# Decoder step: last rows, index projection, both scorings, projections and selection as one stage of interleaved streams

## The reference

```python
h = _rmsnorm(x, p['norm_mix'])
proj = h @ p['w_in']
q, k, v, q_idx, k_idx, w_idx, rw, gate_a, gate_b = _split(proj, SPLIT_SIZES)
...
def _indexer_scores(q_idx, w_idx, k_idx):
    dots = jnp.einsum('bthd,bsd->bths', q_idx, k_idx).astype(jnp.float32)
    w = w_idx.astype(jnp.float32) * IDX_SCALE
    return jnp.einsum('bths,bth->bts', jax.nn.relu(dots), w)
...
past_idx_k = cache_idx_k[page_table].reshape(b, past, IDX_DIM)
all_idx_k = jnp.concatenate([past_idx_k, k_idx.astype(past_idx_k.dtype)], axis=1)
scores = _indexer_scores(q_idx, w_idx, all_idx_k)
scores = jnp.where(causal[None], scores, -jnp.inf)
_, sel = lax.top_k(scores, topk)
...
return x, k, v, k_idx, wkv_new, h[:, -1]
```

## Time and profile before

| what | value |
|---|---|
| median of 3 runs | 3078.86 us (3068.66 to 3085.59) |
| profiled execution, its own time | 3064.48 us |
| its span | 3062.7 us |
| mean granted TensorE clock | 0.904 |
| TensorE busy | 2546.5 us, 83% of the span |
| VectorE busy | 1477.4 us, 48% |
| ScalarE busy | 547.5 us, 18% |
| projection matmuls (L322) | 1248 records, 390.1 us busy |
| counts of the search (L768) | 180 records of the prompt's tiles, 170.3 us busy |

### The profile page before, as it was taken

How to read it: one execution, slowest core, us unless ns; L and a number is a source line. 1 busy time by engine, 2 the same in 40 slices (tenths; PEclk the granted TensorE clock), 3 DMA queues, 4 the chain that set the end, 5 groups by cost and what they waited for, 6 DMA issues and landing times. The chain is left out here.

```text
span 3062.7 us, 52996 instructions
## 1 busy us (share of the span) xinstructions
PE 2546.5 (83%) x21845; PEld 1844.2 (60%) x21845; DVE 1477.4 (48%) x2991; ACT 547.5 (18%) x1139; POOL 76.8 (3%) x120
## 2 busy tenths in 40 slices
PE   4645889994778788787857787799999999999998
PEld 3324556662454555555535454477888888888886
DVE  2142099996427236163344454467554353443443
ACT  3020000001223022231233343321210010000101
POOL 0000000001000000000010010000000000000000
PEclk7865999997988889879879889999999999999999
DMA  3111332223212223132166556353111111111111
GB/s 117 37 48 41 109 112 71 71 64 105 82 44 83 61 59 84 46 86 55 27 208 207 164 186 222 101 201 113 42 40 39 39 38 40 41 41 42 42 42 66
DMA packets 281095, 253.69 MB, mean 83 GB/s; under 512 B 52395, under 2 KB 231181, under 8 KB 280742
## 3 DMA queue, kind: packets, MB, share of 16 engines
q1 hardware_dynamic: 206430, 192.74, 20.4%
q10 hardware_dynamic: 74440, 57.74, 6.4%
HBM read 201.84 MB, written 48.59 MB: 82 GB/s over the span
## 5 line engine op out<-in xcount | busy, mean ns | idle before, releaser
L322 PE MATMUL ps_pr<-hT,w_pr 128*128 128x384 f32 (+1 forms) x1248 | 390.1, 476 | 21.4 <-DMA w_pr<-in_w_in 21.4
L322 PEld LDWEIGHTS ps_pr<-hT,w_pr 128*128 128x128 f32 x1248 | 239.5, 192 | 172.0 <-issue 17.1
L1014 PE MATMUL rwkv_banks<-h_chunk,w_gate 128*128 128x384 f32 (+1 forms) x768 | 290.6, 523 | 18.7 <-ACT gate_rows L1355 8.5
L2497 DVE TENSOR_TENSOR x<-x,ps_mm 128x272 f32<-128x272 f32 x280 | 120.9, 436 | 308.0 <-PE ps_mm L2464 307.9
L2464 PE MATMUL ps_mm<-merged_then_hidden,w_mm 128*128 128x272 f32 x960 | 227.1, 393 | 1.6 <-DVE sums_of_right_sides L2714 0.9
L1014 PEld LDWEIGHTS rwkv_banks<-h_chunk,w_gate 128*128 128x128 f32 x768 | 152.9, 210 | 111.0 <-issue 46.6
L2464 PEld LDWEIGHTS ps_mm<-merged_then_hidden,w_mm 128*128 128x128 f32 x960 | 182.2, 190 | 39.9 <-DVE sums_of_right_sides L2714 1.3
L2464 PE MATMUL ps_mm<-v_T_and_gates_then_h_mlp,w_mm 128*128 128x272 f32 x864 | 204.5, 392 | 0.0
L2488 ACT COPY merged_then_hidden<-ps_mm 128x272 f32<-128x272 f32 x160 | 61.5, 385 | 723.4 <-PE ps_mm L2464 723.4
L2464 PEld LDWEIGHTS ps_mm<-v_T_and_gates_then_h_mlp,w_mm 128*128 128x128 f32 x864 | 164.1, 190 | 33.9
L768 DVE TENSOR_SCALAR_CACHE_REDUCE above<-scores,mid 128x384 f32<-128x384 f32 (+1 forms) x180 | 170.3, 946 | 6.4
(11 more groups left out here) (437 smaller groups left out, 3794.8 us busy)
## 6 DMA issues: line engine op xcount, KB each, us to landing
k_pages<-in_cache_k SPq DMA_DIRECT2D x128, 256.0 KB, 3.1
v_pages<-in_cache_v SPq DMA_DIRECT2D x128, 256.0 KB, 3.9
w_gate<-in_w_in ACTq DMA_DIRECT2D x48, 512.0 KB, 4.2
w_mm<-in_w_mlp_in SPq DMA_DIRECT2D x32, 512.0 KB, 4.9
w_mm<-in_w_mlp_out SPq DMA_DIRECT2D x32, 512.0 KB, 4.8
proj_T<-stage_pr ACTq DMA_DIRECT2D x26, 548.0 KB, 4.0
w_pr<-in_w_in SPq DMA_DIRECT2D x25, 512.0 KB, 3.9
v_T_and_gates_then_h_mlp<-gates_T SPq DMA_DIRECT2D x16, 544.0 KB, 4.7
```

The lines of the kernel that those rows point to most:

```text
L322: ins = self.nc.tensor.matmul(self.ps[0:width, slot % 2, c, 0:m], w[:, k, 0:width], rhs[:, k, t0:t0 + m], start=(k == 0), stop=(k == slice ...
L1014: ins = MM(B[:, GB, 0:w], gw[:, n % 2, k, :], hc[:, k, 0:w], start=(k == 0), stop=(k == KO - 1))
L2497: self.nc.vector.tensor_tensor(to, to, ps, ALU.add).then_inc(self.by_dve, 1)
```

## The change

The five stages `shift_rows`, `project_index`, `score_new`, `score_past` and `project_and_select` become one, `project_score_select`, with one barrier at its end. Its parts on each engine are streams that `weave` puts into one order. The numbers are in steps of roughly a microsecond of projection work: CHUNK = 4.9 for a projection chunk, NEW = 46 for the first unit of the new keys and 0.75 for each further one, PASTS = 84 for the first sequence and 5 for each further one.

- All 29 projection blocks run in one series, the index key block first. They have two PSUM banks in place of two sets of three, and are copied out chunk by chunk (`made` and `kept` count chunks). A chunk is issued in two halves of 4 slices, between which other streams may step.
- The index key rows and index queries stay in SBUF (`kw`, `qi`); the keys for both halves of the partitions, and the small operands of the past scoring, still come back from `proj_T`.
- The units of the new keys are cut at 512 keys: 44 in place of 28, with a ring of four banks.
- All 128 index pages have a buffer of their own, and their loads wait for no earlier sequence; two of three are issued by SP, one of three by ACT. `ties` and `rank` of the selection reuse that memory.
- The pages of a sequence are turned in two groups of 4 transposes, each copied out by itself.
- The last rows are copied by ScalarE instead of VectorE. The bias products follow the first chunks; the store of `hT` is issued late in the stage.
- The loops are written out instead of running on the chip. The bisection loop on VectorE and the masks are as before, and come after all scoring on VectorE's queue.

```diff
-            p.stage(shift_rows, o["shift_prompt"], o["shift_sample"])
-            p.stage(project_index, a["w_in"])
-            p.stage(score_new, o["idxk_prompt"], o["idxk_sample"])
-            p.stage(score_past, a["cache_idx_k"], a["page_table"])
-            p.stage(project_and_select, a["w_in"], a["rel_bias"], one_hot)
+            p.stage(project_score_select, a["w_in"], a["rel_bias"], one_hot, o["idxk_prompt"], o["idxk_sample"],
+                    a["cache_idx_k"], a["page_table"], o["shift_prompt"], o["shift_sample"])
...
+    SLOTS, RING = 4, 4
+    pages = sb("idx_pages", [128, NB, NPG * 64])
+    flat = pages.rearrange("p b c -> p (b c)")
+    ties, rank = flat[:, 0:NKS], flat[:, NKS:2 * NKS]
+    B = p.ps("first_banks", [128, 8, 512], own)
+    blocks = [(col(W_KI, 68), 68, B_KI)] + [(col(W_QI + 128 * j), 128, B_QI + j) for j in range(2)]
+    units = [(i, h, c, min(512, (i + 1) * 128 - c)) for i in SEARCHED for h in range(IH)
+             for c in range(0, (i + 1) * 128, 512)] + [(NI, h, 0, TS) for h in range(IH)]
+    BY_ACT = [g for g in range(NPG) if g % 3 == 2]
+    BY_SP = [g for g in range(NPG) if g % 3 != 2]
+    CHUNK, NEW, ITEM, PASTS, BATCH = 4.9, 46.0, 0.75, 84.0, 5.0
...
+        @block.sync
+            def weights():
+                for n, (parts, _, _) in enumerate(blocks):
+                    yield -1.0 if n < SLOTS else 3 * CHUNK * (n - SLOTS + 1) + 0.2
+                    if n >= SLOTS:
+                        sp.wait_ge(S["made"], 3 * (n - SLOTS + 1))
...
+            def key_pages():
+                yield 0.0
+                sp.wait_ge(S["pt_in"], 16)
+                for n, (b, g) in enumerate((b, g) for b in range(NB) for g in BY_SP):
+                    yield 1.1 * n
+                    load_page(sp, b, g, 0)
+            def once():
+                yield -2.0
+                sp.dma_start(pt[:, :], page_table.rearrange("b (o g) -> o (b g)", o=1)).then_inc(S["pt_in"], 16)
+                yield -0.5
+                sp.dma_start(oh[:, :], one_hot).then_inc(S["nb_in"], 16)
+                sp.dma_start(rb[:, :], rel_bias).then_inc(S["nb_in"], 16)
+                yield 12.0
+                sp.wait_ge(S["last_kept"], 1)
...
+                yield 18.0
+                sp.wait_ge(S["kw_stored"], 16)
...
+                yield 26.0
+                sp.wait_ge(S["kw_rows"], 3)
...
+                yield NEW + 1.0
+                sp.wait_ge(S["q_stored"], 32)
...
+                yield PASTS + NB * BATCH + 20.0
+                sp.dma_start(p.h_d.rearrange("k p t -> p k t"), p.hT[:, :, 0:NT]).then_inc(S["h_kept"], 16)
+            weave(once(), weights(), key_pages())
...
+        @block.tensor
+            def project():
+                    for c, (t0, m) in enumerate(CHX):
+                        q = 3 * n + c
+                        for half in range(2):
+                            yield CHUNK * (q + 0.5 * half)
+                            if half == 0 and q >= 2:
+                                pe.wait_ge(S["kept"], q - 1)
+                            for k in range(4 * half, 4 * half + 4):
+                                ins = MM(B[0:width, 6 + q % 2, 0:m], wk[:, k, 0:width], p.hT[:, k, t0:t0 + m],
+                                         start=(k == 0), stop=(k == KO - 1))
...
+            def bias():
+                    yield 5.0 + 0.5 * n
...
+            def turn_last():
+                yield 10.0
...
+            def turn_kw():
+                    yield 17.0 + 1.2 * g
...
+            def dots_new():
+                for u, (i, h, c, n) in enumerate(units):
+                    yield NEW + ITEM * u
...
+                    if u >= RING:
+                        pe.wait_ge(S["relued"], u - RING + 1)
...
+            def past():
+                for b in range(NB):
+                    for half in range(2):
+                        yield PASTS + BATCH * b + 1.2 * half
+                        turn_pages(b, half)
+                    yield PASTS + BATCH * b + 3.0
+                    dots_past(b)
+                for q in range(NPG // 4):
+                    yield PASTS + BATCH * NB + 4.0 + 2.0 * q
...
+            weave(project(), bias(), turn_last(), turn_kw(), dots_new(), past())
...
+        @block.scalar
+            def keep():
+                    for c, (t0, m) in enumerate(CHX):
+                        yield CHUNK * (q + 1) + 0.05
+                        act.wait_ge(S["made"], q + 1)
...
+            def key_pages():
+                for n, (b, g) in enumerate((b, g) for b in range(NB) for g in BY_ACT):
+                    yield 1.2 * n
+                    load_page(act, b, g, 1)
+            def relu():
+                    yield NEW + ITEM * u + 0.3
+                    act.wait_ge(S["dotted"], u + 1)
+                    if u >= RING:
+                        act.wait_ge(S["added"], u - RING + 1)
...
+            def keep_keys():
+                        yield PASTS + BATCH * b + 1.2 * half + 0.6
...
+            weave(keep(), keep_last(), key_pages(), relu(), keep_keys())
```

More of the change, by code:

```diff
@@ L265, in _ @@
             chain_.wait()
[L268 to L333, removed]
@@ L336 @@
[L336 to L349, removed]
-        for c, (t0, m) in enumerate(d.chunks):
-            ins = self.nc.scalar.copy(self.stage[0:rows, b, t0:t0 + m], d.ps[0:rows, b, c, 0:m])
-            ins.then_inc(d.taken[b] if c == 2 else self.copied, 1)
-        act.wait_ge(self.copied, d.nth(n, 1) * 2 + 2)
-        act.wait_ge(d.taken[b], d.nth(n, 2, 1))
-        dst = self.p.proj[ds(block, 1), 0:rows, :].rearrange("b p t -> (b p) t")
-        act.dma_start(dst, self.stage[0:rows, b, :]).then_inc(self.stored[b], 16)
@@ new lines, in _ @@
+            MM = nc.tensor.matmul
+            def project():
+                loads = [0] * SLOTS
+                for n, (parts, width, _) in enumerate(blocks):
+                    loads[n % SLOTS] += len(parts)
+                    wk = w[:, n % SLOTS, :].rearrange("p (k c) -> p k c", k=KO)
+                    for c, (t0, m) in enumerate(CHX):
+                        q = 3 * n + c
+                        for half in range(2):
+                            yield CHUNK * (q + 0.5 * half)
+                            if c == 0 and half == 0:
+                                pe.wait_ge(w_ready[n % SLOTS], 16 * loads[n % SLOTS])
+                            if half == 0 and q >= 2:
[3 more added lines that the diff above has]
+                                         start=(k == 0), stop=(k == KO - 1))
+                        ins.then_inc(S["made"], 1)
@@ new lines, in turn_pages @@
+            def turn_pages(b, half):
+                if half == 0:
+                    pe.wait_ge(page_in[b][0], 16 * len(BY_SP))
+                    pe.wait_ge(page_in[b][1], 16 * len(BY_ACT))
+                if b == 0:
+                    pe.wait_ge(S["relued"], NU)
+                else:
+                    pe.wait_ge(S["kt_made"], 2 * b + half - 1)
+                for j in range(4 * half, 4 * half + 4):
+                    ins = nc.tensor.transpose(B[:, half, (j % 4) * 128:(j % 4) * 128 + 128],
+                                              pages[:, b, j * 128:j * 128 + 128], p.ident[:, :])
+                ins.then_inc(S["pages_turned"], 1)
@@ L575, in batch @@
                     o = s * 256 + (g // 2) * 32
-                    ins = nc.tensor.matmul(dots[:, g % 2, o:o + 32],
-                                           kt[r0:r0 + 64, s, (g // 2) * 128:(g // 2) * 128 + 128],
-                                           qws[r0:r0 + 64, s, 0:32], start=True, stop=True)
-                ins.then_inc(dotted, 1)
-            for s in range(2):
-                batch(s, s, 0)
-            with pe.Fori(1, NB // 2) as i:
-                for s in range(2):
-                    batch(i * 2 + s, s, i)
```

541 lines of the change are left out of this document (214 added, 327 removed).

## The result

The changed kernel took 2991.32 us in the median of 4 runs (2989.19 to 3000.68), the kernel before 3078.56 in 4. The ratio is 0.9721, with a 95% interval of 0.9696 to 0.9746: 87 us less, where 85 were forecast (2994). The profiled execution took 2992.02 us with a span of 2990.1, only 72.6 less than the profiled span of before. The stages after RWKV took 2.5 us less.

A forecast was written before the change was run, and what follows sets the result against it. VectorE's 345 us search, needing all scores and starting late, was taken to bound the region. 292.3 + 5.6 + 345.3 + 7.0 = 650.2 instead of 735.7, 85.5 us less, gives 2994 us on the median; forecast 2978 to 3010, wider range 2972 to 3034.

The forecast's parts named there:

- Start: First projection matmul, with weight loads issued straight behind the first barrier: at about 93 us instead of 98.3.
- The queue up to the last scores: TensorE's work before the last scores are turned back: 195.3 us plus 4 of small waits, ending at 292.3.
- a batch: Past scoring of one sequence on TensorE: 8 transposes 1.07 us, dots 1.8 (half the low-clock 3.62), together 2.9.
- batches 6 and 7: Last page batches, no half chunk between transposes and dots: TensorE waits for ScalarE's copy, twice about 1.0 us.
- the 55 half chunks: Projection work on TensorE's queue before the last scores: 2.46 us each, 135.1 in all, warm-up 1.9 apart.
- VectorE: After the last turn back: 5.6 us of copies, reductions and causal term, then the unchanged search of 345.3 us.
- The end of the stage: From the last mask to the next stage's first load: 7.0 us, as in the kernel before.
- TensorE's end: 119 half chunks left after the last scores take 293 us; TensorE ends at 585, 58 us short of being last.
- Queues that hand their waits to TensorE: Rival, in the scoring: one late copy stops all streams, about half the gain, 3034 us; 0.20 together with late pages.
- Pages that arrive late: Rival, in the batches: SP's weight waits gate page loads, 3014 to 3034 us; 0.20 together with queue waits.
- bank cycling: Rule against the forecast: changing PSUM banks every chunk idles TensorE, its clock swings, kernel slower; fallen-clock chance 0.04.
- A fallen clock: Rival, in the scoring part: all at 1.2 GHz makes 195 us 390, the time 3189 us; chance 0.04.

The follow-up runs named there:

- more_semaphores: The changed kernel with 40 more unused semaphores allotted to the stage, which its end clears: 2990.72 us in one run.
- the second trace: The changed kernel without an edit, measured again with a trace of a second execution: 2986.87 us, 0.9702 of the kernel before.
- twenty_rounds: The changed kernel with 20 rounds of bisection in place of 30: 2933.05 us, 0.9533 of the kernel before.
- scores_bare: The changed kernel with projection chunks from the tenth on moved behind the whole scoring: 2974.84 us, 0.9673 of the kernel before.
- one_per_batch: The changed kernel with other sort keys, 37 half chunks (not 55) before the last scores, one in each batch: 2944.81 us, 0.9566 of the kernel before.
- bias_first: The kernel before with all eight bias products made ahead of the first projection block: 3057.36 us, 0.9935 of the unedited one.
- pages_ahead: The kernel before with an index page buffer for each of the eight sequences: 3077.23 us, 0.9996 of the unedited one.
- fewer_between: The changed kernel with other sort keys, 43 half chunks (not 55) before the last scores: 2956.98 us, 0.9611 of the kernel before.

## Why the prediction was right

The mechanism is the one forecast: the search starts 84.8 us earlier, takes as long as before, and TensorE ends before it. By the prediction's steps, forecast against trace:

- **Start**: 93 against 90.68. The page table's load costs SP 0.25 us, and the first matmul follows the first weights' issue by 3.4 us instead of 5.0. That block has 68 columns in place of 128; whether that is the reason was not tried.
- **The queue up to the last scores**: 199.3 against 202.3, and its end 292.3 against 292.98, since it began 2.3 sooner. Its terms, from each group's start to the next one's: score matmuls 22.7 against 20.8, in the lower half of the bounds; a batch 2.9 against 2.8 (0.87 of transposes and 1.91 of dots), so halving the low-clock dots was right; bias 6.7 against 6.5; batches 6 and 7 wait 0.67 each, not 1.0; idle time 3.4 in all, where I took 6.0 in two terms. The term that I had too small is the one that looked surest. After the others the 55 half chunks take 145.7 us with the warm-up, where I had 137.0. Between other streams a half chunk takes 2.69 (384 columns, 228.29 to 230.98) or 2.30 (328), 2.56 in the mean of a block, not the 2.46 of the undisturbed stretch behind (119 in 292.25 us); that is 5.5 us. Dips of the clock, 0.97 in the mean of the stretch, are the rest. So this term was 8.7 us too small, and it was made up by the start (2.3), the idle time (2.6), the score matmuls (1.9) and some smaller ones. That the end came within 0.7 us of the forecast is luck.
- **VectorE**: 5.6 and 345.3 us against 5.6 (292.98 to 298.59) and 345.4.
- **The end of the stage**: 7.0 against 9.05. Here the step itself was incomplete: I took the old barrier's price, and it holds a clearing of semaphores whose number the change raises. more_semaphores shows the price.
- **The next stage**: 650.2 against 653.05, and 655.6 in the second trace.
- **TensorE's end**: 585 against 585.06, and its 58 us of room against the 61 us that twenty_rounds took out.

The forecast of 2994 was made on the median. The sum on the single profiled execution, 2979, is 13 us below the 2992 that the profiled execution took; 2.9 of that are the region, most of the rest the RWKV stage's spread, which had been at its short end in the trace of before (808.0). The forecast range is not the one that its bounds give: dots 6 either way and waits from -4 to +21 around 2994 are 2984 to 3021, not 2978 to 3010. The measured time lies in both.

**The rivals.** Queues that hand their waits to TensorE (0.20) didn't come: 3.4 us of waits. ScalarE was the nearest to it. Its page loads put it behind for the first nine chunks, which shows as the waits of 1.4 us for the first score unit and 0.5 for a chunk's bank. Pages that arrive late didn't come either. As for bank cycling, two banks are cycled every 4.9 us, and behind 293 us the trace has no idle time of TensorE at the changes (290.00 us busy of 290.00) and a clock of 1.00. The rule of the Trainium skill ("TensorE: Matmul & The Clock Gate", section "A second HAM failure mode: psum-queue depth-cycling") speaks of a TensorE that falls idle between its groups; that doesn't happen here, so this queue doesn't test it. Nor did the 0.96 of the old stage that I had set against it: from 323 to 720 us TensorE's only wait there is one of 9.7 us for weights.

A fallen clock is a real danger all the same. scores_bare has 0.50 over all eight batches with nothing between them, one_per_batch 1.00 with one half chunk in each. That supports what I had argued from today's 0.52, that the projections in between hold the clock up. What first brings the clock down stays open: in scores_bare, as in the stage before, TensorE came to the batches from idle time.

The runs don't take the change apart fully. bias_first and pages_ahead try two of its parts alone. What keeping the keys in SBUF, the 44 units or the split copies are worth by themselves was not measured.

**What stood in the text and was too small**: that what stands ahead of the last scores costs its own time and hides waits. fewer_between and one_per_batch show that, as long as a half chunk or so remained in each batch, the others hid next to nothing. scores_bare shows the other end: with none left, half of their time came back, more of it by the clock than by waits.

## What to carry to other kernels

When one engine's long job needs the end of another engine's queue, list what stands ahead of that end, price each item, and keep there only what fills a wait or keeps the clock; here 12 and then 6 more half chunks moved behind it were worth some 30 and 12 us. Look at the second-latest engine before you count a gain: moving the search alone by 60 us brought 22. Compare kernels by medians and by stage borders in the trace, not by two profiled spans, when a stage that nobody touched varies by 15 us.

## What the runs showed of the hardware

- TensorE at 84% busy with small matmuls (128 by 128 transposes and dots of 32 columns), after a stretch in which it was busy for 2.16 of 6 us, stayed at a granted clock of 0.50 for 57 us (scores_bare). With one half chunk per batch (eight records of 384 or 328 columns), begun at 1.00, it stayed at 1.00, and the batch with it was shorter (5.4 against 6.20 us).
- Score matmuls with 64 rows of weights, whose heads alternate between the two halves of the partitions, took 20.8 us for 17,152 columns, 1.21 ns each; a projection with 128 rows takes 1.68.
- A semaphore that the end of a stage clears costs 0.066 us (40 of them, 2.63 us, in one run).
- An index page's load (its number read into a register, then the issue) holds a queue for 1.0 to 1.1 us (16 in 16.55 on ScalarE's, 64 in 70.82 on SP's in pages_ahead), and a wait for pages stays when the buffers are free (42.2 of 46.8 us).
